# Hybrid decoder step on one core: a longer tile-by-tile end of the down projection, and four transpositions moved behind the last sample values

## What is computed

```python
proj = h @ w_in                                   # q, k, v of two mixers
oa = attend_a(qa, ka, va)                         # dilated windows, 8 heads x 64
ob = rms_norm(attend_b(qb, kb, vb, lam), subln_g) * (1 - lam_init)   # differential, 4 heads x 128
mixed = concat([oa, ob]) @ w_o
x = layer_norm(ALPHA * x + gate1 * mixed, ln1_g, ln1_b)
h = x * (1 + scale2) + shift2
u = h @ w_up + b_up
uc = b_conv + sum(ext[:, j:j + S] * w_conv[j] for j in range(3))
a, g = split(uc)
y = (gelu(a) * g) @ w_down + b_down               # w_down: 2816 x 1024
x = layer_norm(ALPHA * x + gate2 * y, ln2_g, ln2_b)
```

## Time and profile before

| what | value |
|---|---|
| median of 3 runs | 1189.41 us |
| lowest, highest | 1185.26, 1194.31 us |
| profiled execution, its time | 1186.03 us |
| its span | 1184.3 us |
| TensorE (PE) busy | 1035.5 us, 87% |
| VectorE (DVE) busy | 811.4 us, 69% |
| GpSimd (POOL) busy | 453.3 us, 38% |
| ScalarE (ACT) busy | 271.0 us, 23% |
| mean granted TensorE clock | 0.94 |

### The profile page before, as it was taken

How to read it: one execution, slowest core, us unless ns; L and a number is a source line. 1 busy time by engine, 2 the same in 40 slices (tenths; PEclk the granted TensorE clock), 3 DMA queues, 4 the chain that set the end, 5 groups by cost and what they waited for, 6 DMA issues and landing times.

```text
span 1184.3 us, 24024 instructions
## 1 busy us (share of the span) xinstructions
PE 1035.5 (87%) x9389; PEld 836.7 (71%) x9389; DVE 811.4 (69%) x1485; ACT 271.0 (23%) x600; POOL 453.3 (38%) x575
## 2 busy tenths in 40 slices
PE   4599899994888888879878969999999999999993
PEld 2377657773666666656576759999999998776772
DVE  1637445625886778887867584675867677997868
ACT  0300000001343333343442032323232223000001
POOL 0423223304244444434305034555656566323323
PEclk8699989997998998999988988999999999999997
DMA  8948899969899999999934151677766523314102
GB/s 294 408 158 310 299 356 348 331 212 315 287 348 382 297 343 361 359 342 343 354 134 141 45 181 50 231 254 287 255 248 215 213 72 108 119 59 146 54 1 80
DMA packets 101030, 276.54 MB, mean 234 GB/s; under 512 B 9608, under 2 KB 33174, under 8 KB 97317
## 3 DMA queue, kind: packets, MB, share of 16 engines
q1 hardware_dynamic: 85701, 223.56, 53.9%
q0 software_dynamic: 15168, 51.39, 12.3%
q10 hardware_dynamic: 48, 0.05, 0.0%
HBM read 264.60 MB, written 76.69 MB: 288 GB/s over the span
## 4 chain that ended last, share of the span: by engine, by line
PE 57%; DVE 15%; DMA 10%; issue 9%; SPq 4%; POOL 3%; POOLq 1%; ACT 0%; ACTq 0%; DVEq 0%; PEldq 0%
PE wide L1685 16%; PE wide L1687 15%; PE wide L1686 15%; DVE ring L1239 3%; DMA ring<-in_cache_k 3%; DMA ring<-in_w_ada 2%; DMA room<-in_w_ada 2%; PE wide L1821 2%; PE wide L1633 1%; DMA ring<-in_w_down 1%; PE wide L1765 1%; SPq L636 1%; SPq L464 1%; DVE ring_r L1163 1%; PE wide L1754 1%
## 5 line engine op out<-in xcount | busy, mean ns | idle before, releaser
L812 POOL TENSOR_TENSOR ring_r<-ring,ring_r 128x1024 fp32r<-128x1024 f32 x70 | 180.4, 2585 | 243.2 <-DVE ring_r L1123 205.2
L1685 PE MATMUL wide<-x_sb_r,ring_r 128*128 128x288 f32 x704 | 210.7, 299 | 10.6 <-DVE ht_r L1145 7.5
L1686 PE MATMUL wide<-ht_r,ring_r 128*128 128x288 f32 x704 | 209.0, 297 | 0.0
L1687 PE MATMUL wide<-x_sb_r,ring_r 128*128 128x288 f32 x704 | 208.4, 296 | 0.0
L1685 PEld LDWEIGHTS wide<-x_sb_r,ring_r 128*128 128x128 f32 x704 | 133.1, 189 | 13.5 <-issue 13.5
L1239 DVE STREAM_TRANSPOSE ring<-ring 128x512 f32<-128x512 f32 x208 | 129.3, 679 | 15.7 <-DMA ring<-in_cache_k 15.2
L1687 PEld LDWEIGHTS wide<-x_sb_r,ring_r 128*128 128x128 f32 x704 | 133.9, 190 | 0.0
L1686 PEld LDWEIGHTS wide<-ht_r,ring_r 128*128 128x128 f32 x704 | 133.4, 189 | 0.0
L1687 PE MATMUL wide<-ring_r,ht_r 128*128 128x512 f32 (+1 forms) x336 | 133.2, 396 | 0.0
L1685 PE MATMUL wide<-ring_r,x_sb_r 128*128 128x512 f32 (+1 forms) x240 | 98.3, 409 | 9.0 <-DVE ht_r L1145 8.5
L1686 PE MATMUL wide<-ring_r,x_sb_r 128*128 128x512 f32 (+1 forms) x240 | 95.7, 399 | 0.0
(11 more groups left out here) (241 smaller groups left out, 1954.4 us busy)
## 6 DMA issues: line engine op xcount, KB each, us to landing
ring<-in_cache_k SPq DMA_DIRECT2D x128, 256.0 KB
out_wks<-in_cache_win_k SPq DMA_DIRECT2D x8, 4080.0 KB, 19.1
out_wvs<-in_cache_win_v SPq DMA_DIRECT2D x8, 4080.0 KB, 19.9
ring<-in_w_up SPq DMA_DIRECT2D x22, 1024.0 KB, 7.3
room<-in_w_ada SPq DMA_DIRECT2D x8, 2048.0 KB, 10.3
ring<-in_cache_win_k SPq DMA_DIRECT2D x16, 1024.0 KB
x_sb<-in_cache_v POOLq DMA_DIRECT2D x60, 256.0 KB, 5.8
room<-in_cache_v POOLq DMA_DIRECT2D x56, 256.0 KB, 5.6
```

Of the source, the lines that this page charges most:

```text
L812: nc.gpsimd.tensor_tensor(rest, w, high.bitcast(F32), ALU.subtract).then_inc(wl_rest, 1)
L1685: nc.tensor.matmul(out, left[0], right[0], start=first, stop=False)
L1686: nc.tensor.matmul(out, left[0], right[1], start=False, stop=False)
L1687: return nc.tensor.matmul(out, left[1], right[0], start=False, stop=last)
```

## The change

Two independent edits. First, `turn_mixed(4)` to `turn_mixed(7)` with their wait for `rms_ok` leave the last unit's loop over its value groups and stand behind the sums; on ScalarE `take_out` of the last unit stands ahead of `take_mixed(4)`. Second, in the second half of the down projection the row blocks that go tile by tile are the last ten (f = 12 to 21, `TAIL = 12`) and no longer the last six. Since all ten must lie ready at once, their split parts get places of their own, in `gt` itself, which is read for the last time in this half: the high part of block f goes to the place of block f - 12, whose last split is done, and the rest replaces block f. These ten splits wait for no `g_used`.

```diff
+        TAIL = 12
+
+        def gated(z):
+
+            half, f = divmod(z, FT)
+            if half and f >= TAIL:
+                return part(room_r, (f - TAIL) * NT, NT), part(room_r, f * NT, NT)
+            return g_high_r[:, z % NG_BUF, :], g_rest_r[z % NG_BUF]
...
                 take_mixed(f)
             act.wait_ge(rms_sq, 1)
             nc.scalar.activation(rms[:, 1, :], rms[:, 0, :], ACT.Sqrt).then_inc(rms_rt, 1)
+            take_out(len(sa) - 1)
             for f in range(4, KT_D):
                 take_mixed(f)
-            take_out(len(sa) - 1)
...
             def split_gated(z):
 
-                f, b = z % FT, z % NG_BUF
-                if z >= NG_BUF:
+                f = z % FT
+                if NG_BUF <= z < FT + TAIL:
                     dve.wait_ge(g_used, z - NG_BUF + 1)
-                then(nc.vector.tensor_copy(g_high_r[:, b, :], gt[:, f, :]))
-                nc.vector.tensor_tensor(g_rest_r[b], gt[:, f, :], g_high_r[:, b, :].bitcast(F32), ALU.subtract)\
-                    .then_inc(g_split, 1)
+                high, rest = gated(z)
+                then(nc.vector.tensor_copy(high, gt[:, f, :]))
+                nc.vector.tensor_tensor(rest, gt[:, f, :], high.bitcast(F32), ALU.subtract).then_inc(g_split, 1)
...
                     weigh_group(w, g)
                     if g == 1 and w + 1 < len(sa):
                         prompt_step(PER * w + 3)
-                    if g == 1 and w + 1 == len(sa):
-                        pe.wait_ge(rms_ok, 1)
-                        for f in range(4, KT_D):
-                            turn_mixed(f)
...
             last.then_inc(sa_l, 1)
+
+            pe.wait_ge(rms_ok, 1)
+            for f in range(4, KT_D):
+                turn_mixed(f)
...
-                steps = [(f, t) for f in range(16) for t in range(TP + 1)]
+                steps = [(f, t) for f in range(TAIL) for t in range(TP + 1)]
                 if half == 0:
-                    steps += [(f, t) for f in range(16, FT) for t in range(TP + 1)]
+                    steps += [(f, t) for f in range(TAIL, FT) for t in range(TP + 1)]
                 else:
-                    steps += [(f, t) for t in range(TP + 1) for f in range(16, FT)]
+                    steps += [(f, t) for t in range(TP + 1) for f in range(TAIL, FT)]
...
-                    last = product(bk(j % 8)[0:rows, :], (g_high_r[:, z % NG_BUF, cols], g_rest_r[z % NG_BUF][:, cols]),
+                    high, rest = gated(z)
+                    last = product(bk(j % 8)[0:rows, :], (high[:, cols], rest[:, cols]),
                                    pair_of(n, f % 8), f == 0, f == FT - 1)
```

## The result

The changed kernel took 1176.21 us (median of 4 runs, 1174.91 to 1181.03) against 1187.34 for the kernel before: ratio 0.9896, 95% interval 0.9861 to 0.9930, so 12.3 us less (8.3 to 16.5). The ratio is estimated from the single runs and is not the quotient of the two medians, which are 11.1 us apart. The forecast was 9.7 us less and 1179.5 us, counted from the 1189.41 us known then.

The account below looks back on a forecast made before the run. TensorE was taken to bound the kernel except before the output projection and at the down product's end. Gains of 5.0 + 4.7 = 9.7 us from the 1189.41 us median gave 1179.5 us, range 1172.5 to 1187.

Parts of the forecast that it names:

- The bound and the two places: TensorE bounds the kernel, except at the turn from sample attention to output projection and at the down product's end.
- part 1: Turns behind the last values, before the output projection: gates end earlier and w_o is no longer waited for; 5.0 us gained.
- Part 2: Ten blocks tile by tile at the down product's end: 5.9 less 1.2 us of waiting, 4.7 us gained.
- The delay of VectorE's last tile: End of down product: VectorE's last addition begins 0.08 us behind TensorE's end, not 6.02; worth 5.9 us.
- The wait in the first tile: Start of the ten-block tail: VectorE's splits up to block 21 come 1.3 us late; 1.2 us of waiting taken.
- The 12.33 us behind: From the start of VectorE's last tile addition to the span's end: 12.33 us, claimed to stay.
- I take full clock for the turns: 1.9 us: Before the gates: after a pause of 0.8 us the 16 turns run at full clock, in 1.9 us.
- the lower bound: Part 1 if the clock is low for the turns but recovers as before: 4.1 us are left.
- rival (d): Clock at 1.2 GHz from the turns through gates and selection: part 1 -6.3 us, a loss of 1.6 in all, 1191; 4%.
- (a): Down product's tail: the last weights' load takes 14.0 us, leaving a gain of 2.5 us, 1187; chance 6%.
- (b): Output projection: another release does not move and takes part 1 back; 4.7 us left, 1184.7; chance 9%.
- (c): Down product's tail: VectorE stays behind by the same 6 us, taking part 2 back; 5.0 us left, 1184.4; chance 9%.

Follow-up runs that it names:

- e4: The changed kernel with nine row blocks tile by tile in place of ten (TAIL = 13); 1174.70 us, ratio 0.9881 to the kernel before.
- e6: The changed kernel with the last weight chunk's three high parts made by ScalarE, not VectorE; 1177.46 us, ratio 0.9921 to the kernel before.
- e7: The changed kernel with the first half's additions of tiles 0 and 1 placed behind earlier splits; one run, 1173.48 us.
- e8: The changed kernel with the convolution state's load issued before SyncE waits for the sample values; one run, 1174.64 us.
- e2: The changed kernel with the first edit (the turns) undone, leaving the ten-block tail; 1184.43 us, ratio 0.9956 to the kernel before.

## Why the prediction was right, point by point

**The bound and the two places.** Right. The up product is as long in every trace (295.5 to 297.6 us to the down product's start, before 296.3), so what part 1 had gained at its start was still there at its end.

**Part 2** came out by its own terms. The delay of VectorE's last tile was put at 6.02 less 0.08: it fell to 0.03. The wait in the first tile was put at 1.2 to 1.3 us by the splits of blocks 17 to 21: it was 1.36, for blocks 19 to 21, with the split of block 17 in 5.5 us beside GpSimd; e4 and e6 take it away in two different ways and both gain 1.35. The 12.33 us behind stayed. The sum was put at 4.7; the traces without a low stretch show 4.6 (91.24 to 86.60).

**Part 1** had the right mechanism and one term of the wrong size: "I take full clock for the turns: 1.9 us". The turns took 3.1 to 3.6 us in five of eight traces. I had argued from a pause of 0.69 us that left the clock at 1.00; the pause here was 0.9 to 1.1 (forecast: 0.8), and behind six matmul groups of only 16 columns. Where the clock stayed up (e4, e7, e8) the gates ended 5.4 us sooner than before (19.81 against 25.24), a little more than the 5.1 forecast; where the turns were slow 4.2 to 4.4, near the 4.1 of the lower bound (against e2, with 24.31 at the old place, all of these are 0.9 less); in the changed kernel's first trace, with the gates slow as well, 3.05. That last is the beginning of rival (d), which priced the same stretch at the low clock: it happened for 16 of 64 gate matmuls and cost 1.7 us. On the mean of the six traces with part 1, pauses and the old place of the state load, the state's transposition comes 3.4 us sooner than in the two without part 1 (43.6 against 47.0). At the gates' end the same means are 4.0 us apart (20.8 against 24.8): 0.6 us are lost between, because the load of the state, which I had moved along unchanged, took 8.9 us on the mean of the six against 8.3. Why it takes longer is open. At the up product 3.0 us are left (109.5 against 112.4), mostly because four of the six have the low stretch behind that load (see e8), and one of the two.

**The rivals.** (a) The last weights were there when VectorE had waited 1.65 us: their load landed in 6.8 us, and in 6.7 to 6.9 in all fourteen traces, not in 14. (b) Nothing in the output projection stood still: the state load is on the path, as e8 shows, and moved along, less 0.6 us. (c) VectorE kept pace, even at 6.12 us a tile in e4. (d) Held in part, above.

**The sum.** The traces give 3.4 (at the state) + 4.6 = 8.0 us, or 7.6 with the 3.0 at the up product; the forecast was 9.7, the two measured ratios say 12.3 (8.3 to 16.5) and 10.1 (7.5 to 12.7), and the two parts alone 5.4 and 5.2. All intervals hold the forecast. By the traces part 1's term was too high (5.0 for 3.0 to 3.4), which the ratios, several us wide, cannot show; so the closeness of the total to the forecast may be in part luck. Whether the 2 to 4 us between the traces' sum and the ratios are real stays open: traces are single executions, and the turns of blocks 0 to 3 stand anywhere from 591.5 to 604.3 us in them, in code that no kernel here changes. I had put 0.75 on a change within 1%; the first ratio is 1.04% and the second 0.85%, so the gain sits on that line, as the prediction had said of 9.7 us, though it put too little on the other side of it.

## What to carry to other kernels

When an engine ends late because it gets tiles faster than it can finish them, lengthen the tile until the feeder's share has reached the other's (here 27 matmuls, 6.12 us, for 6.13), and no further: here the tenth block made the first tile wait 1.36 us for its operands. Ask then who prepares the first tile, and move that to an idle engine. When a wait is moved off the path, cost what remains behind it at both clock levels, since TensorE's clock was low behind pauses of about 1 us in some executions, and in none of four with cheap matmuls in them.

## What the runs showed of the hardware that I had not expected

Behind pauses of about 1 us TensorE's clock is sometimes low and sometimes not, with the same code at that place: behind a pause of 0.9 to 1.1 us the 16 turns took 1.97 us in three traces and 3.1 to 3.6 in five; behind two pauses of 0.9 us or more at the start of half two, seven or eight matmuls stood 0.43 us apart in five of eleven traces; behind the wait of 2.2 to 3.4 us for the state, 1.6 us were lost in seven of eleven. The Trainium skill (TensorE: Matmul & The Clock Gate, Part 1) says that the clock is gated by recent activity and that the point of change varies from run to run; these traces agree in that the same code sits at one level in some executions and at the other in others. A price for such a pause is a price with a chance.

VectorE's operations beside GpSimd's took about as long as GpSimd's (2.3 to 2.7 us), small as they were: 2.40 us for one column per row, 2.66 for a cast of 0.45, 2.83 for a subtraction of 0.76. That had gone into the forecast as a term. It alone doesn't make the wait in the first tile: e6 still has three such operations and no wait, with VectorE's own wait for the weights and its high parts gone.
